# Attention's weighted values of a hybrid MLA and mLSTM layer: one fp32 matmul a key tile, or three over rounded parts and rests

## The chip, the cores and the metric

The kernel runs on one core of one Trainium2 chip. The metric is the device time of one execution in microseconds (us). Before the change it is 2083.89 us, the median of three runs (2079.58 to 2084.59).

## The reference, cut to what matters

One layer of a streaming encoder takes 256 prompt frames, 32 sample frames and 16 meta tokens of width 4096. All branch inputs are column blocks of one projection with `w_in`. One branch is latent attention with 16 heads, the other an mLSTM with 4 heads; both are gated, and `w_out` projects them back. The part that the change touches is the last line of the attention:

```python
kv = (ckv @ w_kv_up).reshape(B, S, MLA_HEADS, QK_NOPE + V_HEAD)
k_nope, v = rmsnorm(kv[..., :QK_NOPE], k_nope_norm), kv[..., QK_NOPE:]
s = (jnp.einsum('bqhd,bshd->bhqs', q_nope, k_nope)
     + jnp.einsum('bqhd,bsd->bhqs', q_pe, k_pe)).astype(jnp.float32) * ATTN_SCALE
s = jnp.where(mask[None, None], s, -jnp.inf)
p = jax.nn.softmax(s, axis=-1).astype(v.dtype)
return jnp.einsum('bhqs,bshd->bqhd', p, v)
```

A head has 288 queries. They attend to 432 keys at most, and each head's values are 128 wide.

## The kernel before, in words

Nothing is left to a planner. Each engine has its own instruction list, written out in program order, and the lists meet only in semaphores. The stages are named phases (`PHASES`), and PSUM is used as eight banks, each with a counter of fills (`full`) and one of releases (`free`).

The large projections take their weights in units of 128 rows. SyncE loads raw fp32 weights. ScalarE (`unit`, L668 to L676) rounds a unit to the type fp32r (`whi`), VectorE (`unit`, L1081 to L1086) subtracts the rounded part from the raw one (`wlo`), and TensorE multiplies three times (`mm3`, L1613): rounded by rounded, rounded by rest, rest by rounded. Four slots hold split units. `steps` (L641) puts the split of unit k+3 ahead of the hook of unit k, so each engine does other work only in hooks at fixed unit numbers.

The attention of pair j (heads 2j and 2j+1) lies in such hooks while TensorE runs the 16 up-projection units of pair j+1: 12 for the queries, then 4 for keys and values. The last pair lies beside the 32 units of the first mLSTM projection (phase `ml0qk`). The hooks of a pair, by unit:

- TensorE (L1880 to L1898): k=2 sums of squared keys, k=5 scores of the first head, k=8 scores of the second (the first score matmul waits until bank 4 is free), k=9 and 12 the transposes of the probabilities, k=11 and 13 `weighted`, k=14 sums of squared queries of the next pair.
- VectorE (L1306 to L1327): k=1 scales queries, k=2 and 3 normalise keys, k=5 and 8 row maxima, k=7 and 10 reciprocals of the row sums (`inverse`; the one at k=7 frees bank 4), k=10 and 12 `pt_minor`, which copies a part of the transposed probabilities out of bank 7; k=11 copies of the next queries, k=12 rests of their squares.
- ScalarE (L874 to L892): k=2 the keys' factors, k=6 and 10 exponentials, k=10 and 12 `pt_main`, which copies 320 columns out of bank 6, k=12 and 13 the attended values out of bank 5.
- GpSimd (L2156 to L2164): multiplies the probabilities by the reciprocals.

The values of a pair stand in `vt` from the end of the pair's projection (L816). `weighted` (L1867) multiplies fp32 `vt` by fp32 `probT`, per head in four matmuls of 288, 192, 96 and 32 moving columns. Each fp32 matmul is two records in the trace:

```python
for t, q0, w, at in ((0, 0, 288, 0), (1, 64, 192, 320), (2, 192, 96, 512), (3, 256, 32, 288)):
    ins = mm(bank[5][:, q0:q0 + w], vt[:, t, vh], probT[:, at:at + w], start=t == 0, stop=t == 3,
```

Of the kernel before, what the change touches and what calls it, by code (L numbers as in the profile page):

```python
# [10 lines left out]
MLA_HEADS, NOPE, V_HEAD = 16, 128, 128  # L11
# [17 lines left out]
P = 128  # L29
# [94 lines left out]
def use(phase, bank, nth=0, i=0):  # L124

    before, uses = BASE[phase]
    return before[bank] + nth + i * uses[bank]
# [67 lines left out]
def hymba_step(nc, x_prompt, x_sample, cache_ckv, cache_kpe, state_C, state_n, state_m, meta, norm_gain,  # L195
# [3 lines left out]
    f32, f32r = mybir.dt.float32, mybir.dt.float32r  # L199
    ALU, ACT, AX = mybir.AluOpType, mybir.ActivationFunctionType, mybir.AxisListType  # L200
# [3 lines left out]
    with ctx:  # L204
        def keep(stack):
            return lambda name, shape, dt=f32: stack.enter_context(nc.sbuf_tensor(name, shape, dt))

        def sem(name):
            return ctx.enter_context(nc.semaphore(name))
# [6 lines left out]
        con = sb("con", [P, CONST_COLS])  # L216
# [35 lines left out]
        sb2 = keep(p2)  # L252
# [8 lines left out]
        qpm = [sb2(f"qpm{h}", [P, SEQ + WIDE]) for h in range(2)]  # L261
        kn = sb2("kn", [P, 2, NKX])
        vt = sb2("vt", [P, 4, 2 * V_HEAD])
        ps = ExitStack()
        sqb = keep(ps)("sqb", [P, 3 * NQ])
        rsb = keep(ps)("rsb", [P, 3 * NQ])
# [9 lines left out]
        gsc = sb2("gsc", [P, 2])  # L276
        pa = ExitStack()
        prob = keep(pa)("prob", [P, PROB_COLS])
        probT = keep(pa)("probT", [P, 608])
        pa.close()  # L280
        pb = ExitStack()
        keep(pb)("prob_", [P, PROB_COLS])
# [82 lines left out]
        bank = [ctx.enter_context(nc.psum_tensor(f"bank{b}", [P, 512], f32)) for b in range(8)]  # L365
        full = [sem(f"bank{b}_full") for b in range(8)]
        free = [sem(f"bank{b}_free") for b in range(8)]
# [25 lines left out]
        qp_c, qp_a, qp_fin = (sem(n) for n in ("qpe_cos", "qpe_added", "qpe_normed"))  # L393
        mx, ex, pn, pt_d = (sem(n) for n in ("neg_max", "exp_done", "probs_normed", "probT_minor"))
        pt_zero, prob_zero, ml_zero = sem("probT_zeroed"), sem("prob_zeroed"), sem("mlstm_zeroed")
        mask_in, gb_in = sem("mask_in"), sem("gate_bias_in")
        r_v, r_abs, r_e, r_l, r_c, r_em = (sem(n) for n in ("row_vec", "row_abs", "row_exp", "row_ln", "ccol_done", "emcol_done"))
        m_out = sem("m_out")
# [254 lines left out]
        def _(act):  # L653
# [111 lines left out]
            def rstd(dst, src, scale, bank_no, used, done):  # L765

                act.wait_ge(full[bank_no], used + 1)
                nc.scalar.activation(dst, src, ACT.Ln, scale=scale, bias=epsc[:, :]).then_inc(free[bank_no], 1)  # L768
                act.wait_ge(free[bank_no], used + 1)
                nc.scalar.activation(dst, dst, ACT.Exp, scale=-0.5).then_inc(done, 1)  # L770
# [73 lines left out]
            def k_rstd(phase, i, j):  # L844
                for t in range(2):
                    b = 6 + t

                    if t == 0:
                        act.wait_ge(q_fin, 2 * j + 2)
                        act.wait_ge(qp_fin, 2 * j + 2)  # L850
                    rstd(rs2[:, t, :], bank[b][:, 0:NKV], 1.0 / NOPE, b, use(phase, b, 0, i), k_rs)

            def exps(phase, i, j, h):

                hh = 2 * j + h
                if not (isinstance(j, int) and j == 0 and h == 0):
                    act.wait_ge(full[7], use(phase, 7, h, i) + 1)
                for t, (b, c0, n) in enumerate(((4, 0, P), (4, 144, P), (5, 0, DEC))):
                    act.wait_ge(mx, 3 * hh + (2, 2, 3)[t])
                    at, w = PROB[t]  # L860
                    nc.scalar.activation(prob[0:n, at:at + w], bank[b][0:n, c0:c0 + w], ACT.Exp,  # L861
                                         bias=nmax[0:n, t:t + 1], accum_out=psum_[0:n, t:t + 1]).then_inc(ex, 1)

            def pt_main(phase, i, j, h):

                hh = 2 * j + h
                act.wait_ge(full[6], use(phase, 6, 1 + h, i) + 1)
                nc.scalar.copy(probT[:, 0:320], bank[6][:, 0:320]).then_inc(free[6], 1)

            def attn_evict(phase, i, j, h):  # L870
                act.wait_ge(full[5], use(phase, 5, 2 + h, i) + 1)
# [2 lines left out]
            def attention(phase, i, j):  # L874
                def hooks(k):
                    if k == 2:
                        k_rstd(phase, i, j)
                    if k == 6:
                        exps(phase, i, j, 0)
                    if k == 10:  # L880
                        pt_main(phase, i, j, 0)
                        exps(phase, i, j, 1)
                    if k == 12:
                        if phase == "step":
                            q_square_hi(phase, i, j + 1)
                        attn_evict(phase, i, j, 0)
                        pt_main(phase, i, j, 1)
                    if k == 13:
                        attn_evict(phase, i, j, 1)
                    if k == 15 and phase == "step":  # L890
                        q_rstd(phase, i, j + 1)
                return hooks  # L892
# [181 lines left out]
        def _(dve):  # L1074
            tt, ts_, stt = nc.vector.tensor_tensor, nc.vector.tensor_scalar, nc.vector.scalar_tensor_tensor
# [201 lines left out]
            def k_norm(j, t):  # L1277
                dve.wait_ge(k_rs, 2 * j + t + 1)
                stt(kn[:, t, NKV:NKX], kn[:, t, 0:N_META], G[:, G_KN:G_KN + 1], rs2[:, t, 0:N_META],
                    ALU.mult, ALU.mult).then_inc(k_fin, 1)  # L1280
                dve.wait_ge(k_fin, 4 * j + 2 * t + 1)
                stt(kn[:, t, 0:NKV], kn[:, t, 0:NKV], G[:, G_KN:G_KN + 1], rs2[:, t, :], ALU.mult, ALU.mult)\
                    .then_inc(k_fin, 1)
# [16 lines left out]
            def pt_minor(phase, i, j, h):  # L1300

                dve.wait_ge(full[7], use(phase, 7, 1 + h, i) + 1)
                nc.vector.tensor_copy(probT[:, 320:512], bank[7][:, 64:256]).then_inc(pt_d, 1)
                nc.vector.tensor_copy(probT[0:48, 512:608], bank[7][0:48, 320:416]).then_inc(free[7], 1)

            def attention(phase, i, j):  # L1306
                def hooks(k):
                    if k == 1:
                        q_scale(j)
                    if k in (2, 3):  # L1310
                        k_norm(j, k - 2)
                    if k == 5:
                        maxima(phase, i, j, 0)
                    if k == 7:
                        inverse(phase, i, j, 0)
                    if k == 8:
                        maxima(phase, i, j, 1)
                    if k == 10:
                        pt_minor(phase, i, j, 0)
                        inverse(phase, i, j, 1)  # L1320
                    if k == KQ - 1 and phase == "step":
                        q_evict(phase, i, j + 1)
                    if k == 12:
                        if phase == "step":
                            q_square_lo(j + 1)
                        pt_minor(phase, i, j, 1)
                return hooks  # L1327
# [282 lines left out]
        def _(pe):  # L1610
            mm, tr = nc.tensor.matmul, nc.tensor.transpose
# [84 lines left out]
            for k in range(NAR_UNITS):  # L1696
# [3 lines left out]
                for q in range(4):  # L1700
                    s = slice(72 * q, 72 * q + 72)
                    kk = 4 * k + q
                    ins = mm3(bank[0][0:72, 0:NT], whi[:, k % HL_SLOTS, s], wlo[:, k % HL_SLOTS, s],
                              xhi[:, kk, :], xlo[:, kk, :], kk == 0, kk == KT - 1, kk == 0)
                ins.then_inc(full[0] if k == NAR_UNITS - 1 else unit_used, 1)
                if k == 2:

                    fill("latent", 5)
                    for t in range(KC):
                        pe.wait_ge(ck_sq, t + 1)  # L1710
                        ins = mm(bank[5][:, 0:NT], ones, sq2[:, t % 2, 0:NT], start=t == 0, stop=t == KC - 1)
                        ins.then_inc(full[5] if t == KC - 1 else ck_ssm, 1)
                if k == 4:
# [3 lines left out]
                    for t in range(KC):  # L1717
                        ins = tr(bank[4][:, t * P:t * P + P], cacher[:, t * P:t * P + P], ident)
# [148 lines left out]
            def weighted(phase, i, j, h):  # L1867

                for b in (1, 2):
                    pe.wait_ge(free[b], use(phase, b, 0, i))  # L1870
                pe.wait_ge(free[6], use(phase, 6, 1 + h, i) + 1)
                pe.wait_ge(free[7], use(phase, 7, 1 + h, i) + 1)
                fill(phase, 5, 2 + h, i)
                vh = slice(P * h, P * h + P)
                for t, q0, w, at in ((0, 0, 288, 0), (1, 64, 192, 320), (2, 192, 96, 512), (3, 256, 32, 288)):
                    ins = mm(bank[5][:, q0:q0 + w], vt[:, t, vh], probT[:, at:at + w], start=t == 0, stop=t == 3,  # L1876
                             skip_group_check=True)
                ins.then_inc(full[5], 1)

            def attention(phase, i, j):  # L1880
# [21 lines left out]
            pe.wait_ge(barred_in, 16 * 4)  # L1902
            pe.wait_ge(qn_zero, 1)
            pe.wait_ge(prob_zero, 1)
            pe.wait_ge(pt_zero, 1)
            for j in range(0, 7):
                q_units(j + 1, "step", j, attention("step", j, j))
                kv_units(j + 1, "step", j, attention("step", j, j))
# [188 lines left out]
        def _(pool):  # L2097
            tt, ts_ = nc.gpsimd.tensor_tensor, nc.gpsimd.tensor_scalar
# [66 lines left out]

            q_square("bulk0", 0, 0)

            nc.gpsimd.memset(probT[:, 512:608], 0.0).then_inc(pt_zero, 1)
            nc.gpsimd.memset(prob[:, :], 0.0).then_inc(prob_zero, 1)
            k_square("bulk0", 0, 0)  # L2170
            q_turn("bulk0", 0, 0)
# [80 lines left out]
```

## Time and profile before

| what | value |
|---|---|
| median of three runs | 2083.89 us |
| the profiled execution, its own time | 2084.3 us |
| its span | 2082.5 us |
| TensorE busy | 2060.5 us, 99% |
| VectorE, ScalarE, GpSimd busy | 52%, 44%, 9% |
| granted TensorE clock, mean | 1.0 |
| attention of the eight pairs | about 283 to 569 us |

The span is what the profiler covers; the own time contains the 1.8 us around it. Matmul records overlap, since they are pipelined: what one of them takes from TensorE is the distance between its start and the next one's, not its duration. The share of an engine is an average, and says nothing of the few places where TensorE waits.

### The profile page before, as it was taken

What the parts mean: (1) busy time and instruction counts of PE and PEld (TensorE: products, weight loads), DVE (VectorE), ACT (ScalarE), POOL (GpSimd) and SP (SyncE); (2) the same over time, 40 slices, a digit from 0 to 9 for tenths busy, and PEclk for the clock granted to TensorE, in tenths of its full rate; (3) what the DMA queues carried; (4) which work ended last, traced back from release to release, by engine and by line L of the source; (5) the groups of instructions that cost most, each with busy time, mean ns of one, the idle gap of its engine ahead of it and who ended that gap; (6) DMA issues with size and microseconds to landing.
All of it is one profiled execution on the core that took longest, in us unless ns stands there. A gap on an engine that the chain in (4) does not pass through costs nothing.

```text
span 2082.5 us, 36420 instructions
## 1 busy us (share of the span) xinstructions
PE 2060.5 (99%) x15123; PEld 2026.0 (97%) x15123; DVE 1090.9 (52%) x1986; ACT 919.6 (44%) x1837; POOL 180.1 (9%) x205
## 2 busy tenths in 40 slices
PE   7999999999999999999999999999999999999999
PEld 7999999999999999999999999999999999999999
DVE  4545666666555445454455555444455654444444
ACT  4644455555444334343344444444444543333333
POOL 0001033332300000000000000000001000000000
PEclk9999999999999999999999999999999999999999
DMA  9655442323365454554545656555555555555554
GB/s 220 183 170 154 116 121 84 107 82 115 106 173 142 135 169 126 166 144 133 164 130 165 170 163 168 166 164 169 163 162 165 170 182 183 184 184 184 183 184 135
DMA packets 195925, 321.96 MB, mean 155 GB/s; under 512 B 20948, under 2 KB 66672, under 8 KB 195712
## 3 DMA queue, kind: packets, MB, share of 16 engines
q1 hardware_dynamic: 193424, 315.50, 52.6%
q10 hardware_dynamic: 2336, 4.13, 0.6%
q8 instruction: 120, 1.97, 0.4%
q14 instruction: 45, 0.37, 0.1%
HBM read 309.95 MB, written 9.62 MB: 153 GB/s over the span
## 4 chain that ended last, share of the span: by engine, by line
PE 93%; DVE 3%; ACT 2%; DMA 1%; issue 1%; SPq 0%; POOL 0%; DVEq 0%; ACTq 0%
PE bank L1615 29%; PE bank L1619 28%; PE bank L1618 28%; DVE wlo L1085 1%; PE bank L1876 1%; DMA xt<-in_x_prompt_dram 1%; PE bank L1772 1%; PE bank L1769 1%; PE bank L1771 1%; DVE sqr L1249 1%; PE bank L2087 0%; ACT whi L675 0%; ACT rsb L768 0%; ACT prob L861 0%; PE bank L1841 0%
## 5 line engine op out<-in xcount | busy, mean ns | idle before, releaser
L1085 DVE TENSOR_TENSOR wlo<-raw,whi 128x512 fp32r<-128x512 f32 (+1 forms) x1256 | 810.2, 654 | 910.7 <-ACT whi L675 907.8
L675 ACT CAST whi<-raw 128x512 fp32r<-128x512 f32 (+1 forms) x1256 | 710.0, 577 | 1010.9 <-PE bank L1619 965.0
L1615 PE MATMUL bank<-xhi,whi 128*128 128x288 f32 (+2 forms) x3104 | 928.7, 299 | 0.7 <-DVE wlo L1085 0.7
L1619 PE MATMUL bank<-xhi,wlo 128*128 128x288 f32 (+2 forms) x3104 | 922.2, 297 | 0.0
L1618 PE MATMUL bank<-xlo,whi 128*128 128x288 f32 (+2 forms) x3104 | 921.0, 297 | 0.0
L1615 PEld LDWEIGHTS bank<-xhi,whi 128*128 128x128 f32 (+1 forms) x3104 | 581.9, 187 | 3.6 <-issue 1.1
L1618 PEld LDWEIGHTS bank<-xlo,whi 128*128 128x128 f32 (+1 forms) x3104 | 582.1, 188 | 1.3 <-issue 1.0
L1619 PEld LDWEIGHTS bank<-xhi,wlo 128*128 128x128 f32 (+1 forms) x3104 | 582.1, 188 | 0.0
L1615 PE MATMUL bank<-mhi,whi 128*128 128x288 f32 x1024 | 303.3, 296 | 0.0
L1618 PE MATMUL bank<-mlo,whi 128*128 128x288 f32 x1024 | 302.7, 296 | 0.0
L1619 PE MATMUL bank<-mhi,wlo 128*128 128x288 f32 x1024 | 300.9, 294 | 0.0
L1619 PEld LDWEIGHTS bank<-mhi,wlo 128*128 128x128 f32 x1024 | 192.6, 188 | 0.0
L1618 PEld LDWEIGHTS bank<-mlo,whi 128*128 128x128 f32 x1024 | 192.2, 188 | 0.0
L1615 PEld LDWEIGHTS bank<-mhi,whi 128*128 128x128 f32 x1024 | 192.1, 188 | 0.1
L1615 PE MATMUL bank<-cqhi,whi 128*128 128x288 f32 x288 | 89.5, 311 | 1.3 <-ACT vt L816 0.7
L1619 PE MATMUL bank<-cqhi,wlo 128*128 128x288 f32 x288 | 84.9, 295 | 0.0
L1618 PE MATMUL bank<-cqlo,whi 128*128 128x288 f32 x288 | 84.9, 295 | 0.0
L1615 PEld LDWEIGHTS bank<-cqhi,whi 128*128 128x128 f32 x288 | 54.1, 188 | 4.4 <-DVE wlo L1085 2.1
L1618 PEld LDWEIGHTS bank<-cqlo,whi 128*128 128x128 f32 x288 | 54.2, 188 | 0.1
L1619 PEld LDWEIGHTS bank<-cqhi,wlo 128*128 128x128 f32 x288 | 54.1, 188 | 0.0
L2164 POOL TENSOR_SCALAR prob<-prob,pinv 128x144 f32<-128x144 f32 (+2 forms) x48 | 41.0, 867 | 117.7 <-DVE pinv L1297 117.7
L2194 POOL TENSOR_TENSOR E<-E,mask 128x464 f32<-128x464 f32 x4 | 4.8, 1190 | 461.4 <-ACT E L961 461.4
(312 smaller groups left out, 1487.8 us busy)
## 6 DMA issues: line engine op xcount, KB each, us to landing
raw<-in_w_in_dram SPq DMA_DIRECT2D x316, 512.0 KB, 3.8
raw<-in_w_out_dram SPq DMA_DIRECT2D x128, 512.0 KB, 3.7
raw<-in_w_in_dram SPq DMA_DIRECT2D x140, 256.0 KB, 3.1
raw<-in_w_q_up_dram SPq DMA_DIRECT2D x48, 384.0 KB, 3.3
raw<-in_w_kv_up_dram SPq DMA_DIRECT2D x16, 512.0 KB, 3.7
xres<-in_x_prompt_dram SPq DMA_DIRECT2D x16, 256.0 KB, 4.0
out_dram<-ytok SPq DMA_DIRECT2D x15, 256.0 KB, 4.4
xt<-in_x_prompt_dram SPq DMA_DIRECT2D x7, 384.0 KB, 9.0
```

The source lines that it names most:

```text
L675: ins = nc.scalar.copy(hi, src)
L1085: ins = tt(lo, src, hi.bitcast(f32), ALU.subtract)
L1249: tt(ksl[:, t, :], sq2[:, t, :], ksh[t].bitcast(f32), ALU.subtract).then_inc(k_sql, 1)
L1615: ins = mm(out, w_hi, m_hi, start=start, stop=False, **kw)
L1618: mm(out, w_hi, m_lo, start=False, stop=False, **kw)
L1619: return mm(out, w_lo, m_hi, start=False, stop=stop, **kw)
L1769: mm(out, ckhi[:, k, cs], vcols(whi), start=k == 0 and half == 0, stop=False, skip_group_check=True)
L1771: mm(out, cklo[:, k, cs], vcols(whi), start=False, stop=False, skip_group_check=True)
L1772: ins = mm(out, ckhi[:, k, cs], vcols(wlo), start=False, stop=last, skip_group_check=True)
L1876: ins = mm(bank[5][:, q0:q0 + w], vt[:, t, vh], probT[:, at:at + w], start=t == 0, stop=t == 3, skip_group_check=True)
L2164: ts_(prob[0:n, at:at + w], prob[0:n, at:at + w], pinv[0:n, t:t + 1], None, ALU.mult).then_inc(pn, 1)
L2194: tt(E[:, 0:464], E[:, 0:464], mask[:, 0:464], ALU.mult).then_inc(e_m, 1)
```

## The change

The values of a pair are split once, at k=4: ScalarE rounds `vt` to `vah`, VectorE subtracts to get `val`, each in two instructions of 128x512. The transposed probabilities are split for each head: the copies out of banks 6 and 7 now write the rounded type (`pth`), and VectorE then reads the banks again and writes the rests (`ptl`) in three subtractions. The release of banks 6 and 7 moves behind these. `weighted` calls `mm3`, so each of the four matmuls becomes three of fp32r operands. GpSimd's clearing of the last 96 columns becomes two multiplications by zero in place of one memset. Three tiles are added.

```diff
+        vah = sb2("vah", [P, 4, 2 * V_HEAD], f32r)
+        val = sb2("val", [P, 4, 2 * V_HEAD], f32r)
+        ptl = sb2("ptl", [P, 608], f32r)
...
-        probT = keep(pa)("probT", [P, 608])
+        pth = keep(pa)("pth", [P, 608], f32r)
...
-                nc.scalar.copy(probT[:, 0:320], bank[6][:, 0:320]).then_inc(free[6], 1)
+                nc.scalar.copy(pth[:, 0:320], bank[6][:, 0:320]).then_inc(pth_d, 1)
...
+                    if k == 4:
+                        for half, b in ((0, 1), (1, 2)):
+                            act.wait_ge(free[b], use(phase, b, 0, i))
+                            nc.scalar.copy(vah[:, 2 * half:2 * half + 2, :], vt[:, 2 * half:2 * half + 2, :]).then_inc(vah_d, 1)
...
-                nc.vector.tensor_copy(probT[:, 320:512], bank[7][:, 64:256]).then_inc(pt_d, 1)
-                nc.vector.tensor_copy(probT[0:48, 512:608], bank[7][0:48, 320:416]).then_inc(free[7], 1)
+                hh = 2 * j + h
+                nc.vector.tensor_copy(pth[:, 320:512], bank[7][:, 64:256]).then_inc(pt_d, 1)
+                nc.vector.tensor_copy(pth[0:48, 512:608], bank[7][0:48, 320:416]).then_inc(pt_d, 1)
+                dve.wait_ge(pth_d, hh + 1)
+                tt(ptl[:, 0:320], bank[6][:, 0:320], pth[:, 0:320].bitcast(f32), ALU.subtract).then_inc(free[6], 1)
+                dve.wait_ge(pt_d, 2 * hh + 2)
+                tt(ptl[:, 320:512], bank[7][:, 64:256], pth[:, 320:512].bitcast(f32), ALU.subtract).then_inc(ptl_d, 1)
+                tt(ptl[0:48, 512:608], bank[7][0:48, 320:416], pth[0:48, 512:608].bitcast(f32), ALU.subtract)\
+                    .then_inc(free[7], 1)
...
+                    if k == 4:
+                        for half in range(2):
+                            dve.wait_ge(vah_d, 2 * j + half + 1)
+                            tt(val[:, 2 * half:2 * half + 2, :], vt[:, 2 * half:2 * half + 2, :],
+                               vah[:, 2 * half:2 * half + 2, :].bitcast(f32), ALU.subtract).then_inc(val_d, 1)
...
+                pe.wait_ge(val_d, 2 * j + 2)
                 for t, q0, w, at in ((0, 0, 288, 0), (1, 64, 192, 320), (2, 192, 96, 512), (3, 256, 32, 288)):
-                    ins = mm(bank[5][:, q0:q0 + w], vt[:, t, vh], probT[:, at:at + w], start=t == 0, stop=t == 3,
-                             skip_group_check=True)
+                    ins = mm3(bank[5][:, q0:q0 + w], vah[:, t, vh], val[:, t, vh], pth[:, at:at + w], ptl[:, at:at + w],
+                              t == 0, t == 3, skip_group_check=True)
...
-            nc.gpsimd.memset(probT[:, 512:608], 0.0).then_inc(pt_zero, 1)
+            for pad in (pth, ptl):
+                ts_(pad[:, 512:608], con[:, 0:96], 0.0, None, ALU.mult).then_inc(pt_zero, 1)
```

## Rows read from the trace of the kernel before

**Rows 1.** The page, part 4: the chain that ended last, by engine.

```profile
PE 93%; DVE 3%; ACT 2%; DMA 1%; issue 1%; SPq 0%; POOL 0%; DVEq 0%; ACTq 0%
```

**Rows 2.** Waits, 283 to 575 us: who waited for whom, us, times, longest.

```profile
PE bank L1841 <- DVE pinv L1297: 3.0, 7, 0.4
```

**Rows 3.** TensorE's timeline, both `weighted` of one pair: start, us, what, idle before.

```profile
377.37 0.30 PE L1619 MATMUL bank<-cqhi,wlo 128*128 128x288 f32 x1
377.50 1.34 PE L1876 MATMUL bank<-probT,vt 128*128 128x288 f32 x8
378.67 0.44 PE L1615 MATMUL bank<-ckhi,whi 128*128 128x432 f32 x1
378.95 0.36 PE L1618 MATMUL bank<-cklo,whi 128*128 128x432 f32 x1
...
384.72 1.34 PE L1876 MATMUL bank<-probT,vt 128*128 128x288 f32 x8
386.18 0.36 PE L1618 MATMUL bank<-cklo,whi 128*128 128x432 f32 x1
386.37 0.36 PE L1619 MATMUL bank<-ckhi,wlo 128*128 128x432 f32 x1
```

**Rows 4.** TensorE's timeline, an mLSTM hook with matmuls of 2 moving columns.

```profile
715.62 0.25 PE L2046 MATMUL bank<-ones_r,kwh 128*128 128x2 f32 x1
715.73 0.25 PE L2046 MATMUL bank<-ones_r,kwl 128*128 128x2 f32 x1
715.84 0.38 PE L1615 MATMUL bank<-xhi,whi 128*128 128x288 f32 x1
```

**Rows 5.** VectorE's timeline, units k=3 to 7 of the same pair.

```profile
365.89 0.67 DVE L1282 SCALAR_TENSOR_TENSOR kn<-kn,G,rsb 128x432 f32<-128x432 f32 x1
366.48 1.16 DVE L1085 TENSOR_TENSOR wlo<-raw,whi 128x256 fp32r<-128x256 f32 x4
367.55 0.30 DVE L1288 TENSOR_REDUCE nmax<-bank 128x1 f32<-128x144 f32 x1
...
370.15 0.62 DVE L1085 TENSOR_TENSOR wlo<-raw,whi 128x256 fp32r<-128x256 f32 x2 [1.16 <-ACT whi L675]
370.69 0.16 DVE L1297 RECIPROCAL pinv<-psumrow 128x2 f32<-128x2 f32 x1
```

**Rows 6.** ScalarE's timeline, the same stretch.

```profile
364.47 2.11 ACT L675 CAST whi<-raw 128x256 fp32r<-128x256 f32 x8
368.30 0.38 ACT L861 ACTIVATE prob<-bank,nmax 128x144 f32<-128x144 f32 x1 [1.72 <-DVE nmax L1289]
...
369.52 1.74 ACT L675 CAST whi<-raw 128x256 fp32r<-128x256 f32 x5
```

**Rows 7.** TensorE's timeline, the second head's scores of the same pair.

```profile
370.99 0.48 PE L1841 MATMUL bank<-kn,qn 128*128 128x144 f32 x2 [0.44 <-DVE pinv L1297]
```

**Rows 8.** VectorE's timeline, units k=4 to 7 of the last pair.

```profile
547.20 1.29 DVE L1085 TENSOR_TENSOR wlo<-raw,whi 128x512 fp32r<-128x512 f32 x2
549.18 0.31 DVE L1288 TENSOR_REDUCE nmax<-bank 128x1 f32<-128x144 f32 x1 [0.70 <-PE bank L1842]
...
552.77 0.16 DVE L1297 RECIPROCAL pinv<-psumrow 128x2 f32<-128x2 f32 x1
```

**Rows 9.** TensorE's timeline, the second head's scores of the last pair.

```profile
554.50 0.41 PE L1841 MATMUL bank<-kn,qn 128*128 128x144 f32 x2
```

**Rows 10.** VectorE's timeline, `pt_minor` of both heads, and of a contended pair of subtractions.

```profile
357.71 1.95 DVE L1249 TENSOR_TENSOR sqr<-sqb,ksh 128x432 fp32r<-128x432 f32 x2 [1.18 <-ACT ksh L810]
...
376.72 0.17 DVE L1297 RECIPROCAL pinv<-psumrow 128x2 f32<-128x2 f32 x1 [0.43 <-ACT prob L861]
...
383.00 0.24 DVE L1304 COPY probT<-bank 48x96 f32<-48x96 f32 x1
```

**Rows 11.** Groups of instructions by shape, 283 to 575 us: xcount, busy us, mean ns.

```profile
L1234 DVE TENSOR_TENSOR rope<-bank,con 128x288 f32<-128x288 f32 x8 | 3.6, 447 | 0.0
```

**Rows 12.** GpSimd's timeline after its two memsets.

```profile
282.87 1.99 POOL L2144 TENSOR_TENSOR sqb<-kn 128x432 f32<-128x432 f32 x2 [8.20 <-DVE kn L1260]
```

More of the change, by code:

```diff
@@ L395, in hymba_step @@
         pt_zero, prob_zero, ml_zero = sem("probT_zeroed"), sem("prob_zeroed"), sem("mlstm_zeroed")
+        vah_d, val_d, pth_d, ptl_d = (sem(n) for n in ("v_rounded", "v_rest", "probT_rounded", "probT_rest"))
         mask_in, gb_in = sem("mask_in"), sem("gate_bias_in")
@@ L1904, in _ @@
             pe.wait_ge(prob_zero, 1)
-            pe.wait_ge(pt_zero, 1)
+            pe.wait_ge(pt_zero, 2)
             for j in range(0, 7):
```

## The prediction

> **What bounds the kernel now.** I read the chain of waits first. It runs over TensorE for 93% of the span [rows 1], so what TensorE executes counts one to one, and what the other engines do counts only where TensorE waits for them. The view of waits, cut to the attention, shows the only such place that repeats: the first score matmul of the second head waits seven times for the reciprocals, 3.0 us in all [rows 2], which is 0.44 us each [rows 7]. The eighth pair lies beside longer units and does not wait. Then I read the timelines of one pair, engine by engine, to see what makes that wait. Backwards from TensorE's start at 370.99: reciprocals on VectorE at 370.69, directly behind the split of a unit at 370.15, which had waited 1.16 us for ScalarE [rows 5]; ScalarE's casts from 369.52, directly behind the exponentials that began at 368.30 after 1.72 us of waiting for the maxima [rows 6]; the maxima at 367.55, directly behind four pieces of split weights from 366.48, and these behind the keys' norm from 365.89 [rows 5]. So for some five microseconds ahead of that wait, TensorE's end is set by VectorE and ScalarE, without a gap between the keys' norm and the maxima. TensorE, with its 99% busy, hides this well: the slack of the chain is not small, it is below zero. Anything put on it comes out at TensorE in full.
>
> **The change part by part.**
>
> TensorE, the matmuls. Today one `weighted` takes, measured from the start of the matmul before it to that of the second after it, 378.95 - 377.37 = 1.58 us. Of that 0.13 us is the 288-column neighbour's own distance (377.50 - 377.37) and 0.19 us that of 432 columns (386.37 - 386.18), so the block takes 1.26 us [rows 3]. It becomes twelve single-pass matmuls. Three of them have 288 columns and cost the 0.13 us of that neighbour: 0.39 us. The nine others have 192, 96 or 32 columns, and no fp32r matmul of these widths stands in the trace. Below them stand matmuls of 2 columns with full 128-column weights of their own: their distance is 0.11 us (starts at 715.62, 715.73, 715.84), though two columns are next to no work, so this is the weight load that each needs [rows 4]. I take 0.11 us for all nine, since 192 columns at 0.13 / 288 us each would be 0.087, under that floor too. Sum: 0.39 + 9 x 0.11 = 1.38 us against 1.26, or +0.12 us a head and some +2 us for 16 heads. The change removes a quarter of the column work and pays for it in weight loads. The bounds: without the floor, 3 x 608 columns at 0.13 / 288 us are 0.82 us, -0.44 us a head, -7.0 us in all. If a narrow single pass cost what fp32 costs now (1.26 / 608 = 2.07 ns a column), the block would be 0.39 + 3 x 320 x 0.00207 = 2.38 us, +1.12 a head, +18 us in all.
>
> The Trainium skill has a rule on this floor: the page "TensorE: Matmul & The Clock Gate", section "Back-to-back issue gap", gives about 81 ns a matmul for a sustained stream of load and matmul at 128 columns, and its section "LDWEIGHTS" columns / 1.2, here 107 ns. The trace's 111 ns agrees with the second and not with the first; by the first, the block would be an estimated 1.12 us and the change would win 0.14 us a head, about 2 us, on TensorE.
>
> ScalarE at k=4: two casts of 128x512. Four units of 384 columns take 2.11 us there, so 512 columns take at most 0.70 us and both 1.4 us [rows 6]. They lie between casts that have been finished by 366.58 and the exponentials at 368.30; the 1.72 us of waiting cover them [rows 6]. If that cover failed they would add to the chain what remains. I cost them at nothing.
>
> VectorE at k=4: two subtractions of 128x512. Two instructions of that kind and size in a row take 1.29 us, with single lengths of 0.69, so each takes 0.60 us of the queue [rows 8]: 1.20 us. They stand behind the split of unit 7 and ahead of that of unit 8 and of the maxima, which run there without a gap (366.48, 367.55) [rows 5]. The rounded values are there in time: ScalarE reaches them after its second unit of the four, near 365.5, and ends both by about 366.9, while VectorE comes to them at about 367.0. So maxima, exponentials, the next unit's split and the reciprocals all come 1.20 us later, and behind them waits TensorE, which has nothing else queued: +1.20 us in each of the seven pairs that wait already [rows 2, 7], +8.4 us. Bounds: zero, if the subtractions found idle time; 2.6 us a pair (+18 us), if the casts ended up in the chain as well. In the last pair the maxima wait 0.70 us for TensorE, and the reciprocals stand at 552.77, 1.73 us ahead of TensorE's 554.50 [rows 8, 9]: 1.20 us goes into that, and I count nothing.
>
> VectorE in `pt_minor`: three subtractions a head, out of PSUM, of 320, 192 and 96 columns. The nearest row has 288 columns and 0.447 us [rows 11], of which about 0.09 overlaps with the next, as above; less 0.1 us per 100 columns this gives some 0.39 + 0.26 + 0.16, and with the last one's own tail 0.9 us. The first head's copies end at 376.72 - 0.43 = 376.29, so bank 7 comes free at about 377.15; `weighted` starts at 377.50 and its weight load 0.13 us sooner, so 0.2 us are left [rows 3, 10]. The reciprocals behind them move from 376.72 to about 377.07, as 0.43 us of waiting covers the rest [rows 10]; the second head's probabilities then come 0.35 us later, and so may its `pt_minor`: copies end at 383.24 + 0.35, the subtractions at about 384.5, the weight load at 384.59 [rows 3, 10]. It just fits. I count nothing, and what that costs if it fails is the second rival. The copies themselves keep their length; only their output type changes. TensorE's new wait for `val` is met some nine microseconds earlier.
>
> GpSimd's two clearings in place of one stand ahead of a memset that is followed by 8.20 us of waiting [rows 12]: nothing. No DMA is added or moved.
>
> **Sum.** +2 + 8.4 = +10.4 us on the profiled execution's own 2084.3 us: 2094.7 us. The median of the runs shown is 0.4 us lower, which is within their spread, and I leave the forecast at 2094.7 us.
>
> **The rivals.**
>
> A narrow single pass is no cheaper than today's fp32. For it: no fp32r row between 2 and 256 columns exists, and 2 columns can't show a price per column. Against it: each of the 2-column matmuls is one record, where fp32 has two [rows 3, 4]. It gives 2084.3 + 18 + 8.4 = 2111 us.
>
> The subtractions in `pt_minor` come late. For it: the margins of 0.1 to 0.2 us, and that two subtractions of 432 columns took 1.95 us beside GpSimd's work, where 1.2 would be due [rows 10]; GpSimd works beside the second head's. Stretched by half they would end 0.45 us later and hold TensorE up by some 0.25 us in each of 16 heads: +4 us, 2099 us.
>
> VectorE's values at k=4 are hidden. It would need idle time between the keys' norm and the maxima, which no row shows in the seven pairs, though the last pair has 0.70 us [rows 5, 8]. Then only the matmuls are left: 2084.3 + 2 = 2086.3 us, no change.
>
> The other side: the block is paid by its columns, 0.82 us. The place is `weighted`, the price -7.0 us, and it decides once the reciprocals' delay is under 7.0 / 7 = 1.0 us a pair. With the 1.20 us it gives 2085.7 us, no change; with no delay 2077.3 us, faster. For it speaks that the load of a matmul behind a 288-column one is wholly covered today, since that one's 0.13 us is more than the load's 0.11 [rows 3, 4]; against it, that only three such stand in the block and all nine others are shorter than the load.
>
> **How the numbers follow.** About 0.3% (6.3 us) is what a measurement of this kernel can tell from no change; slower means over 2090.1 us. Forecast 0.66, late `pt_minor` 0.14, costly narrow passes 0.08, values hidden 0.07, paid by columns 0.05 (0.03 of it faster). In the forecast's case a low median leaves 0.04 within the bound. Slower: 0.66 + 0.14 + 0.08 - 0.04 = 0.84; same: 0.07 + 0.02 + 0.04 = 0.13; faster 0.03. The range goes from the hidden values' case, 2086, to 2103, which holds the late `pt_minor` and half of a cast in the chain; the costly narrow passes and most of the last rival are left out.
>
> **What would show it.** In the changed kernel's timeline, the wait of the second head's first score matmul for the reciprocals grows from 0.44 to about 1.6 us in seven pairs, and the maxima start 1.2 us later against the keys' norm. The distances inside `weighted` are 0.133 us three times and 0.11 us nine times. The weight load ahead of `weighted` shows no idle time. The last pair shows no wait. The prediction is wrong if the narrow matmuls are spaced by their columns, or if the reciprocals' wait stays near 0.44 us.

## The result, and the profile after

The changed kernel takes 2095.57 us, the median of four runs (2094.42 to 2096.18), against 2084.24 us for the kernel before, measured again beside it (four runs). The ratio is 1.0061, 95% interval 1.0048 to 1.0073: slower by 11.3 us, where +10.4 us was forecast. The profiled execution has a span of 2094.0 us against 2082.5 us, +11.5 us.

First the waits of TensorE between 283 and 590 us, to be read against [rows 2].

```profile
PE bank L1861 <- DVE pinv L1305: 11.4, 7, 1.6
```

The same seven waits, 11.4 us in place of 3.0: +8.4 us. The timeline of TensorE at one of them [rows 7], and of VectorE ahead of it [rows 5]:

```profile
372.93 0.29 PE L1639 MATMUL bank<-cqhi,wlo 128*128 128x288 f32 x1
374.85 0.36 PE L1861 MATMUL bank<-kn,qn 128*128 128x144 f32 x1 [1.63 <-DVE pinv L1305]
```

```profile
368.56 0.67 DVE L1290 SCALAR_TENSOR_TENSOR kn<-kn,G,rsb 128x432 f32<-128x432 f32 x1
369.14 0.62 DVE L1093 TENSOR_TENSOR wlo<-raw,whi 128x256 fp32r<-128x256 f32 x2
369.68 1.28 DVE L1330 TENSOR_TENSOR val<-vt,vah 128x512 fp32r<-128x512 f32 x2
370.88 0.62 DVE L1093 TENSOR_TENSOR wlo<-raw,whi 128x256 fp32r<-128x256 f32 x2
371.42 0.30 DVE L1296 TENSOR_REDUCE nmax<-bank 128x1 f32<-128x144 f32 x1
```

From the keys' norm to the maxima it was 367.55 - 365.89 = 1.66 us [rows 5]; now it is 371.42 - 368.56 = 2.86 us, and the 1.20 us between are the two subtractions from 369.68 to 370.88. ScalarE's rounding does not show in this chain; it lies in its wait for the maxima, which is there still [rows 6]:

```profile
368.13 1.13 ACT L885 CAST vah<-vt 128x512 fp32r<-128x512 f32 x2
369.17 1.11 ACT L679 CAST whi<-raw 128x256 fp32r<-128x256 f32 x4
372.16 0.38 ACT L865 ACTIVATE prob<-bank,nmax 128x144 f32<-128x144 f32 x1 [1.88 <-DVE nmax L1297]
```

Then `weighted` of the second head of this pair, on TensorE, the start of each matmul first [rows 3]:

```profile
388.70 0.28 PE L1792 MATMUL bank<-wlo,ckhi 128*128 128x256 f32 x1
388.81 0.37 PE L1635 MATMUL bank<-pth,vah 128*128 128x288 f32 x1
389.02 0.29 PE L1638 MATMUL bank<-ptl,vah 128*128 128x288 f32 x1
389.15 0.29 PE L1639 MATMUL bank<-pth,val 128*128 128x288 f32 x1
389.28 0.25 PE L1635 MATMUL bank<-pth,vah 128*128 128x192 f32 x1
389.37 0.27 PE L1638 MATMUL bank<-ptl,vah 128*128 128x192 f32 x1
389.48 0.27 PE L1639 MATMUL bank<-pth,val 128*128 128x192 f32 x1
389.59 0.23 PE L1635 MATMUL bank<-pth,vah 128*128 128x96 f32 x1
389.66 0.27 PE L1638 MATMUL bank<-ptl,vah 128*128 128x96 f32 x1
389.77 0.28 PE L1639 MATMUL bank<-pth,val 128*128 128x96 f32 x1
389.88 0.25 PE L1635 MATMUL bank<-pth,vah 128*128 128x32 f32 x1
389.98 0.26 PE L1638 MATMUL bank<-ptl,vah 128*128 128x32 f32 x1
390.09 0.26 PE L1639 MATMUL bank<-pth,val 128*128 128x32 f32 x1
390.20 0.44 PE L1635 MATMUL bank<-ckhi,whi 128*128 128x432 f32 x1
390.48 0.36 PE L1638 MATMUL bank<-cklo,whi 128*128 128x432 f32 x1
```

The block takes 390.20 - 388.81 = 1.39 us, where it took 1.17. Read the distances: 0.21 us for the first, then 0.13, 0.13; after that 0.11 us whether 192, 96 or 32 columns move, but for the first matmul of each width, which is 0.02 to 0.045 us shorter. The matmul ahead of it is wider, which fits a weight load that began under that one; no run tests this. The last row shows what stays: 0.28 us for a matmul of 432 columns behind the block where 0.19 is due, as before. From one pair's first block to the next pair's, it is 37.75 us, the mean of the six such distances ahead of the last pair, against 36.10 before: +1.65 us a pair. This distance hardly varies within a trace, and tells small effects apart better than the time of the whole kernel does; it is given below where it decides.

### The profile page after: what moved, and what is told of

The parts are those of the page before. It is cut to its first block, busy times and chain, and to the rows that moved or that the text cites. A ratio compares the mean times of both kernels' runs of the same rounds, so it can differ in the third digit from the quotient of the medians.

```text
span 2094.0 us, 36645 instructions
## 1 busy us (share of the span) xinstructions
PE 2064.2 (99%) x15187; PEld 2030.5 (97%) x15187; DVE 1114.0 (53%) x2050; ACT 926.9 (44%) x1853; POOL 182.7 (9%) x206
## 4 chain that ended last, share of the span: by engine, by line
PE 93%; DVE 3%; ACT 2%; DMA 1%; issue 1%; SPq 0%; POOL 0%; DVEq 0%; ACTq 0%
PE bank L1635 29%; PE bank L1639 28%; PE bank L1638 28%; DVE wlo L1093 1%; DMA xt<-in_x_prompt_dram 1%; PE bank L1792 1%; PE bank L1789 1%; PE bank L1791 1%; DVE sqr L1257 1%; PE bank L2108 0%; ACT whi L679 0%; ACT rsb L772 0%; DVE val L1330 0%; ACT prob L865 0%; PE bank L1861 0%
```

## The experiments

The theory has three parts, to be told apart: (a) the values' rests ahead of the maxima, +1.20 us in seven pairs; (b) twelve single passes cost more than four fp32 matmuls, by weight loads; (c) the bank release comes late by little. Each experiment's time stands beside the kernel before, measured again on the same chip.

**The values' split alone.** Added to the kernel before, at k=4 of ScalarE and VectorE, with no reader:

```diff
+    nc.scalar.copy(vah[:, 2 * half:2 * half + 2, :], vt[:, 2 * half:2 * half + 2, :]).then_inc(vah_d, 1)
...
+    tt(val[:, 2 * half:2 * half + 2, :], vt[:, 2 * half:2 * half + 2, :],
+       vah[:, 2 * half:2 * half + 2, :].bitcast(f32), ALU.subtract).then_inc(val_d, 1)
```

> The kernel before with one part of the change alone: the values are rounded by ScalarE and subtracted by VectorE at k=4, but nothing reads the results; the weighted values stay fp32. Theory: the wait of the second head's scores grows by 1.20 us in seven pairs, +8.4 us on the kernel before, about 2092.5 us. Rival (the matmuls carry the loss): the time of before, about 2084 us.

2091.96 us against 2083.85, ratio 1.0039 (1.0024 to 1.0054): +8.1 us. TensorE's waits:

```profile
PE bank L1853 <- DVE pinv L1304: 11.4, 7, 1.6
```

Two casts and two subtractions that nobody reads cost nearly three quarters of the whole loss, and from pair to pair it is 37.31 us, +1.21. That it is the subtractions' place and not the casts is shown further down, where the casts stay at k=4 and the subtractions move. Part (a) is shown.

**The matmuls alone.** The changed kernel without rests:

```diff
-    mm3(bank[5][:, q0:q0 + w], vah[:, t, vh], val[:, t, vh], pth[:, at:at + w], ptl[:, at:at + w],
+    mm3(bank[5][:, q0:q0 + w], vah[:, t, vh], vah[:, t, vh], pth[:, at:at + w], pth[:, at:at + w],
```

> The other part alone: twelve fp32r matmuls a head, but no rest is computed. ScalarE rounds the values as it copies them out of PSUM, the probabilities are only rounded, and the rounded parts stand in for the rests, so the rests' part of the sum is left out. Theory: the block of weighted goes from 1.17 to 1.32 us by itself, 0.144 us for each of 16 heads, +2.3 us on the kernel before, about 2086.5 us; the wait for the reciprocals stays at 0.44 us. Rival (the matmuls are the loss): +11 us, about 2095 us. Rival (three single passes are cheaper than four): under 2084 us.

2086.04 us against 2083.85, ratio 1.0009 (0.9999 to 1.0018). The +2.2 us are not clear of the noise, since the interval holds 1; the trace carries them, with 36.37 us from pair to pair, +0.27. In its block the first distance is the plain 0.13 us, and the block takes 385.27 - 383.95 = 1.32 us, +0.15 us a head:

```profile
383.95 0.29 PE L1620 MATMUL bank<-pth,vah 128*128 128x288 f32 x1
384.08 0.29 PE L1623 MATMUL bank<-pth,vah 128*128 128x288 f32 x1
...
385.27 0.44 PE L1620 MATMUL bank<-ckhi,whi 128*128 128x432 f32 x1
```

**Half of the weight columns.** Is 0.11 us the weight load? The same kernel, with nine matmuls taking 64 columns of weights:

```diff
+    m, vs = (P, vh) if t == 0 else (64, slice(P * h, P * h + 64))
-    mm3(bank[5][:, q0:q0 + w], vah[:, t, vh], vah[:, t, vh], ...
+    mm3(bank[5][0:m, q0:q0 + w], vah[:, t, vs], vah[:, t, vs], ...
```

> The matmuls alone, as in the experiment with rounded parts only, but the nine matmuls of 192, 96 and 32 columns take only the first 64 columns of weights, so that half of the output's rows miss these keys (left out). Theory (a narrow single pass costs its weight load, and that goes by the number of weight columns): the distances of the 96- and 32-column matmuls fall from 0.111 to about 0.056 us, and the block from 1.32 to about 1.0 us, -5 us, about 2081 us. Rival (0.111 us is a floor for each instruction or for the type): no change, 1.32 us and 2086 us.

2081.07 us against 2084.16, ratio 0.9986 (0.9977 to 0.9995), 5.0 us under the kernel with whole weights (by the two comparisons, each with its own runs of before, it is 5.3). The block takes 0.98 us in place of 1.32, and the records of the weight loads in it last 0.13 to 0.14 us for 64 columns, where those of 128 columns last 0.19.

```profile
377.08 0.25 PE L1620 MATMUL bank<-pth,vah 128*64 128x192 f32 x1
377.17 0.25 PE L1623 MATMUL bank<-pth,vah 128*64 128x192 f32 x1
377.26 0.25 PE L1624 MATMUL bank<-pth,vah 128*64 128x192 f32 x1
377.35 0.21 PE L1620 MATMUL bank<-pth,vah 128*64 128x96 f32 x1
377.39 0.22 PE L1623 MATMUL bank<-pth,vah 128*64 128x96 f32 x1
377.45 0.22 PE L1624 MATMUL bank<-pth,vah 128*64 128x96 f32 x1
377.51 0.19 PE L1620 MATMUL bank<-pth,vah 128*64 128x32 f32 x1
```

With half of the weights the 192 columns show their own price, 0.09 us, and the 96 and 32 columns 0.058 us, half of the floor (0.04 for the first of a width). So the floor goes by the number of weight columns, not by the instruction or the type: it is the weight load. The rival in which a narrow single pass costs as much as fp32 by the column had fallen with the distances of 0.11 us themselves.

**The probabilities' rests alone.** Added to the kernel before, behind the copies, with the releases of banks 6 and 7 moved behind them:

```diff
+    tt(ptl[:, 0:320], bank[6][:, 0:320], probT[:, 0:320], ALU.subtract).then_inc(free[6], 1)
+    tt(ptl[:, 320:512], bank[7][:, 64:256], probT[:, 320:512], ALU.subtract).then_inc(ptl_d, 1)
+    tt(ptl[0:48, 512:608], bank[7][0:48, 320:416], probT[0:48, 512:608], ALU.subtract).then_inc(free[7], 1)
```

> The kernel before with the third part of the change alone: VectorE makes the three subtractions out of banks 6 and 7 for each head and releases the banks behind them, but nothing reads the results, the values are not split and the weighted values stay fp32. Theory (the banks come free just at the time at which TensorE's queue reaches the waits, and the late weight load costs 0.07 us a head): the first distance in the block grows from 0.243 to about 0.31 us, about +1 us on the kernel before, 2085 us; the wait for the reciprocals of the first head stays. Rival (the subtractions fit into the slack): the first distance stays 0.243 us and the time that of before, 2084 us.

2085.01 us against 2084.16, ratio 1.0005 (0.9996 to 1.0014): not to be told from no change. The trace tells more, and half against the expectation: in the first heads the block keeps its 1.17 us, in all eight second heads it begins 0.06 to 0.11 us late and takes 1.25 us. From pair to pair it is 36.26 us, +0.16.

```profile
384.56 0.28 PE L1781 MATMUL bank<-wlo,ckhi 128*128 128x256 f32 x1
384.75 1.41 PE L1885 MATMUL bank<-probT,vt 128*128 128x288 f32 x8
386.00 0.44 PE L1624 MATMUL bank<-ckhi,whi 128*128 128x432 f32 x1
```

**The order of TensorE's waits.** In the changed kernel:

```diff
                 for b in (1, 2):
                     pe.wait_ge(free[b], use(phase, b, 0, i))
+                fill(phase, 5, 2 + h, i)
+                pe.wait_ge(val_d, 2 * j + 2)
                 pe.wait_ge(free[6], use(phase, 6, 1 + h, i) + 1)
                 pe.wait_ge(free[7], use(phase, 7, 1 + h, i) + 1)
-                fill(phase, 5, 2 + h, i)
                 vh = slice(P * h, P * h + P)
-                pe.wait_ge(val_d, 2 * j + 2)
```

> The changed kernel with the waits of TensorE ahead of weighted in another order: the one for bank 7, which is met last, stands behind the others and not ahead of two of them. Theory (bank 7 comes free just in time, and the two waits that stand behind it take about 0.1 us each in TensorE's queue, which puts the first weight load 0.07 us late in 15 heads): the first distance in the block falls from 0.206 to about 0.13 us, about -1 us, 2094.5 us. Rival (0.206 us is what the first matmul over a fresh weight type costs): the distance stays, 2095.5 us.

2095.83 us, ratio 1.0055 (1.0039 to 1.0072): the time doesn't show it. The trace does: the pairs follow each other after 37.61 us in place of 37.75, and the first distance falls to 0.131 us in the second heads of seven pairs, but only to between 0.15 and 0.20 in the first heads. In the last pair it stays as it was, 0.13 and 0.21.

```profile
389.22 0.29 PE L1635 MATMUL bank<-pth,vah 128*128 128x288 f32 x1
389.35 0.29 PE L1638 MATMUL bank<-ptl,vah 128*128 128x288 f32 x1
```

So the 0.07 us is lateness and not a price of the type. Why the order cures only the second heads stands in the trace of the changed kernel. VectorE and TensorE's weight load (PEld), in the first head and then in the second:

```profile
380.74 0.24 DVE L1318 TENSOR_TENSOR ptl<-bank,pth 48x96 fp32r<-48x96 f32 x1
380.97 0.13 DVE L1306 RECIPROCAL pinv<-psumrow 32x1 f32<-32x1 f32 x1
381.32 0.19 PEld L1635 LDWEIGHTS bank<-pth,vah 128*128 128x128 f32 x1
...
388.21 0.24 DVE L1318 TENSOR_TENSOR ptl<-bank,pth 48x96 fp32r<-48x96 f32 x1
388.78 0.19 PEld L1635 LDWEIGHTS bank<-pth,vah 128*128 128x128 f32 x1
```

In the second head the last release is bank 7's, by the last subtraction. In the first head it is another one: `weighted` also waits for bank 5 (`fill`), and what frees that is the second head's reciprocal at L1306, which stands on VectorE behind the three subtractions and ends 0.12 us after bank 7's release. TensorE's queue does the rest. From the last release to the weight load pass 0.33 us where two more wait instructions stand behind the one that is met last (the second head above), 0.23 us with one (first heads here, second heads of the run before this one), and 0.115 us with none (last pair here in this run, 578.27 against 578.15): 0.11 us for each. Part (c) is in the traces and too small for the time.

**The values' rests behind the reciprocals.** In the changed kernel, the two subtractions moved from k=4 to behind `inverse` at k=7:

> The changed kernel with one thing moved: VectorE subtracts the values' rests at k=7, behind the reciprocals that release bank 4, where it is idle for 1.3 us until the second head's scores, and no longer at k=4 ahead of the maxima. Theory (the subtractions at k=4 delay the reciprocals for which TensorE waits in seven pairs by 1.20 us each): that wait falls from 1.6 back to 0.44 us and the time by 8.4 us, to about 2087 us. Rival (the loss lies in TensorE's own matmuls and in the late release of bank 7): no change, about 2095.5 us.

2092.54 us against 2083.85, ratio 1.0043 (1.0028 to 1.0058): some 3 us won, not 8.4. The intervals of this kernel and of the changed one overlap; the distance from pair to pair does not leave it open, 37.18 us against 37.75. This miss is mine. TensorE's wait for the reciprocals fell to 3.9 us as expected, but a new one stood beside it:

```profile
PE bank L1860 <- DVE pinv L1305: 3.9, 7, 0.6
PE bank L1876 <- POOL prob L2184: 3.4, 7, 0.5
```

```profile
373.40 3.85 POOL L2184 TENSOR_SCALAR prob<-prob,pinv 128x144 f32<-128x144 f32 x3 [10.87 <-DVE pinv L1305]
```

The reciprocals start GpSimd's three scalings, which take 2.48 us in the kernel before and 3.85 us here, and the transposes of the first head waited for them. The first scaling, beside the two subtractions, grew from 0.80 to 1.47 us; the second by 0.10 us; and the third, which now came so late that it met the split of the next unit on VectorE, from 0.75 to 1.36 us. I had looked for idle time on VectorE, and not at who would work beside it.

**Half a dose.** One subtraction at k=4, the other at k=7:

> Half a dose: one of the two subtractions of the values stays at k=4 ahead of the maxima, the other stands behind the reciprocals at k=7. Theory (what stands ahead of the maxima comes out at TensorE one to one; what stands behind the reciprocals slows GpSimd by its own length): the wait of the second head's scores is 1.6 - 0.6 = 1.0 us, and that of the transposes for GpSimd nearly nil, since one subtraction lengthens the scaling by 0.6 us and the slack is 0.75: about 2091.5 us. Rival (the wait is met by something else once the subtractions are there at all): 1.6 us as in the changed kernel, 2095.5 us.

2090.87 us against 2084.16, ratio 1.0032 (1.002 to 1.0043). The wait for the reciprocals is 7.2 us, 1.0 us a pair, halfway between 3.0 and 11.4 within 0.1 us, and the transposes wait for nothing. The chain passes on what is put on it, one to one.

**The rests in the gap.** At k=6, between the maxima and the unit that waits for ScalarE:

> The changed kernel with the subtractions of the values at k=6, behind the maxima and one split unit, where VectorE waits 1.2 us for ScalarE and GpSimd has not yet begun to scale the probabilities. Theory (the move to k=7 won only 3 of 8.4 us because the subtractions then ran beside GpSimd's scaling and slowed it from 2.48 to 3.9 us, so that the transposes waited for it): the wait of the second head's scores stays near 0.5 us, the wait of the transposes for GpSimd, 0.5 us in seven pairs, is gone, and the time is about 2087 us, some 3 us over the kernel before. Rival (any place behind the maxima costs the same, since VectorE is short of time in each pair): 2092.5 us, as with k=7.

2088.42 us against 2084.03, ratio 1.0019 (1.001 to 1.0028). No wait for GpSimd is left, which shows that the place beside it was part of the cost at k=7. The wait for the reciprocals is 4.1 us, 0.58 each, as the subtractions fill the gap and a little more. What remains, +4.4 us, is (b), (c) and this.

**The kernel before with earlier reciprocals.** One line, on VectorE:

```diff
-                    if k == 7:
+                    if k == 6:
                         inverse(phase, i, j, 0)
```

> The kernel before, with the first head's reciprocals at k=6 and no longer at k=7, so that they no longer stand behind the split of a unit that waits for ScalarE. Theory (the chain of VectorE and ScalarE has no slack and sets TensorE's 0.44 us in seven pairs): the wait goes, -3.0 us on the kernel before, about 2081 us. Rival (TensorE is bound by its own work, and the wait is only moved to a later one): about 2084 us.

2079.39 us against 2084.03, ratio 0.9979 (0.997 to 0.9988). VectorE, then TensorE:

```profile
365.88 0.60 DVE L1085 TENSOR_TENSOR wlo<-raw,whi 128x256 fp32r<-128x256 f32 x2
367.15 0.17 DVE L1297 RECIPROCAL pinv<-psumrow 128x2 f32<-128x2 f32 x1 [0.67 <-ACT prob L861]
```

```profile
367.76 0.29 PE L1619 MATMUL bank<-cqhi,wlo 128*128 128x288 f32 x1
367.89 0.41 PE L1841 MATMUL bank<-kn,qn 128*128 128x144 f32 x2
```

The gain is 4.6 us (by the interval, 2.5 to 6.3), and I had expected the 3.0 us of the view of waits. Idle time is counted from the end of a matmul's record; the next may start long before that end. From start to start the wait cost 370.99 - 370.26 - 0.13 = 0.60 us (the last unit matmul started at 370.26), and seven times that is 4.2 us. From pair to pair it is 35.43 us against 36.10: 0.67 us less, 4.7 us in seven pairs, so the trace bears the larger figure out.

**All of the change, placed by the slack.** Reciprocals at k=6, the values' rests behind them, bank 7's wait last:

> The whole change with its work placed by the slack: reciprocals at k=6, the values' rests behind them, the wait for bank 7 last. Theory: no wait for the reciprocals, so only the matmuls' 2.3 us remain against the 3.0 us of the wait that the kernel before has: about 2083 us. The rests now run beside GpSimd's scaling, but that begins 1.7 us sooner and has this as slack. Rival (the contention with GpSimd holds the transposes up all the same): 2087 us or more.

2081.98 us against 2084.03, ratio 0.9988 (0.9979 to 0.9996), and no wait in the attention but the first pair's 0.7 us for `vt`. The same instructions as the changed kernel, 13.4 us less (each against its own runs of before); GpSimd's scalings are slowed here too (3.50 us), but have begun early enough. Against the kernel before with the same earlier reciprocals it is 2.6 us slower, of which part (b) is 2.3 us.

**Single passes only where they are wide.**

```diff
+                for t, q0, w, at in ((0, 0, 288, 0), (1, 64, 192, 320)):
+                    mm3(bank[5][:, q0:q0 + w], vah[:, t, vh], val[:, t, vh], pth[:, at:at + w], ptl[:, at:at + w],
+                        t == 0, False, skip_group_check=True)
+                for t, q0, w, at in ((2, 192, 96, 0), (3, 256, 32, 96)):
+                    ins = mm(bank[5][:, q0:q0 + w], vt[:, t, vh], ptx[:, at:at + w], start=False, stop=t == 3,
+                             skip_group_check=True)
```

> A version meant to beat both: three single passes only for the matmuls of 288 and 192 columns, the ones of 96 and 32 columns stay fp32; reciprocals at k=6, the values' rests (now one subtraction) behind them, and the wait for bank 7 last. Theory: the block is 3 x 0.131 + 0.09 + 2 x 0.11 for the wide ones and 0.36 for the narrow, 1.06 us against 1.17, -1.7 us for 16 heads, and the wait for the reciprocals, 3.0 us, is gone: about 2079 us. Rival (the change of type inside one block costs a weight load more each time): about 2081 us, no better than the kernel before with the earlier reciprocals.

2077.50 us against 2084.03, ratio 0.9968 (0.9956 to 0.9981): the fastest. The block:

```profile
375.66 0.29 PE L1633 MATMUL bank<-pth,vah 128*128 128x288 f32 x1
...
376.36 0.55 PE L1899 MATMUL bank<-ptx,vt 128*128 128x96 f32 x4
376.75 0.45 PE L1633 MATMUL bank<-ckhi,whi 128*128 128x432 f32 x1
```

It is 1.09 us, under the 1.17 of fp32 throughout. Most of the 6.5 us is the reciprocals' place; the two intervals (this one and that of the kernel before with earlier reciprocals) overlap, so the times alone don't separate the last 1.9 us. The trace has 0.17 us a pair of it, 35.26 against 35.43, which is the two shorter blocks.

## Why the prediction was right

**The chain of VectorE and ScalarE.** Forecast +1.20 us in seven pairs; the wait grew by 1.19 us, the part alone costs 8.1 us, and half of it adds half to the wait. This step carried the prediction. The halved dose and the moved subtractions leave no other place for it. It rested on reading the rows as a chain without a gap, and on the wait that was there already: a wait of 0.44 us, 3.0 us in a kernel that is 99% busy, says that the slack of five microseconds of other engines' work is spent.

**The matmuls.** The mechanism and the floor were right, the term was mis-sized: forecast +0.12 us a head, measured +0.15 with the banks free in time and +0.22 in the changed kernel. The step that slipped was "so the block takes 1.26 us", where the starts give 1.17. That sum held the 0.09 us by which the matmul behind the block is late, while the 1.38 us for the new block did not, though a block that ends in short matmuls leaves it too. In the other direction, the first narrow matmul of each width came 0.02 to 0.045 us cheaper than the floor, 0.08 us a block. The forecast of 1.38 us for the new block was met (1.39) by luck: these 0.08 us and the 0.07 us of lateness cancel, and with the banks free in time it is 1.32. Sum over 16 heads in the changed kernel: 3.4 us and not 2.

**The release of the banks.** I wrote that it "just fits" and counted nothing; 0.07 us a head was lost in 15 of 16 heads. That is a small piece of the rival of late subtractions, not its 0.25 us, since their lengths came out as priced and GpSimd did not slow them (0.472, 0.340 and 0.239 us). Only in the last pair's second head did the block also begin 0.22 us late, which with the 0.07 us is the rival's size, once. Two things were left out of my account of the slack. One is TensorE's own queue, 0.11 us for each wait behind the one that is met last. The other is bank 5: for the first head I counted only bank 7, and moved the second head's reciprocals by 0.35 us without seeing that the first head's block waits for one of them. With the kernel before's matmuls the first heads were just in time, with no further wait behind bank 5's.

**The last pair** did not wait for its reciprocals, as forecast.

**The cost of ScalarE's casts and of GpSimd's two clearings**: nothing, as forecast.

The sum of the parts alone, 8.1 + 2.2 + 0.9 = 11.2 us, is near the 11.3 us measured for the whole, but each part is uncertain by 2 to 3 us, so that agreement proves little. The traces prove more: from pair to pair the parts add 1.21 + 0.27 + 0.16 = 1.64 us, the whole 1.65, and seven times that is 11.5 us, the difference of the spans. The rivals "paid by its columns" and "costly narrow passes" are refuted by the distances of 0.11 us, and "values hidden" by the split alone.

## What to carry to other kernels

A wait of a few tenths of a microsecond on the bounding engine, if it repeats, marks a chain on other engines that has no slack: price every instruction that a change puts on that chain at full length, whatever the busy shares say, and look for the place behind the release that the bounding engine waits for. When such work is moved into a gap, ask who runs beside it there. Three single passes in place of an fp32 matmul pay only where the moving side is wide enough to cover the weight load; here 288 columns gain 0.09 us (0.39 against 0.485), 192 about break even (0.31 against 0.325), 96 and 32 lose 0.10 and 0.15 us. Of several waits ahead of a matmul, put the one that is met last at the end.

## What the runs showed of the hardware

- A single-pass matmul with 128 columns of weights has a floor of 0.111 us between starts, from 2 to 192 moving columns, where its neighbours are no wider; with 64 columns of weights it is 0.058 us. At 32 columns the two records of an fp32 matmul take 0.057 and 0.112 us, 0.17 together, against 0.32 us for three passes.
- Beside VectorE's subtractions of two SBUF operands of 128x512, a scaling in SBUF on GpSimd took 1.47 us instead of 0.80, while the subtractions themselves stayed at 0.66 to 0.67 us. In the kernel before, beside GpSimd's products for the rotated part of the queries (below), it was a subtraction of VectorE that became longer: of two alike [rows 10] the first took 0.81 us and the second 1.22.

```profile
358.13 2.19 POOL L2154 TENSOR_TENSOR qpm<-rope,rsb 64x288 f32<-64x288 f32 x2
```

- The idle time that the view of waits puts down for a matmul understates the loss by the overlap of records: 0.44 us read, 0.60 us from start to start, 0.67 us from pair to pair gained when it was removed.
- A wait instruction that stands in TensorE's queue behind the wait that is met last delays the next weight load by 0.11 us (0.115, 0.23 and 0.33 us from release to load with none, one and two of them).
